# Interleaving the first slabs and computing six norms by square root, reciprocal and a Newton step

## What is computed

```
def rms_norm(x, g):
    xf = x.astype(jnp.float32)
    y = xf * lax.rsqrt(jnp.mean(xf * xf, axis=-1, keepdims=True) + EPS)
    return (y * g.astype(jnp.float32)).astype(x.dtype)

for i in range(DEPTH):              # DEPTH = 2
    h = rms_norm(x, g[0]); h = mlstm_mixer(h, ...) or short_conv_mixer(h, ...)
    x = x + rms_norm(h, g[1])
    h = sqrelu_mlp(rms_norm(x, g[2]), w_mlp_up[i], w_mlp_down[i])
    x = x + rms_norm(h, g[3])
```

## Time and profile before

| what | value |
| --- | --- |
| three runs | 954.48, 957.66, 964.06 us, median 957.66 |
| profiled execution | 954.73 us, of which the span of its instructions 952.9 us |
| mean granted TensorE clock | 0.993 |
| TensorE, VectorE, ScalarE, GpSimd busy | 99%, 68%, 56%, 10% |
| DMA | 172 MB, 181 GB/s |

### The profile page before, as it was taken

One profiled execution on the slowest core, in us unless ns is written; L12 is line 12 of the kernel. 1 busy time (PEld: TensorE's weight loads), 2 busy tenths in 40 slices (PEclk: granted clock), 3 DMA queues, 4 the chain that ended last, 5 costly groups with the idle time before them and its releaser, 6 DMA issues.

```text
span 952.9 us, 20117 instructions
## 1 busy us (share of the span) xinstructions
PE 942.0 (99%) x8046; PEld 934.3 (98%) x8046; DVE 644.4 (68%) x886; ACT 536.6 (56%) x757; POOL 100.0 (10%) x96
## 2 busy tenths in 40 slices
PE   9999999999999999999999999999999999999997
PEld 8999999999999999999999999999999999999997
DVE  5667687665444886688765444894765679999742
ACT  6566667654444555556655444565554566767542
POOL 0111100000000000109100000015120120000001
PEclk9999999999999999999999999999999999999998
DMA  8532646455554365545655553654342445556531
GB/s 330 226 133 94 222 173 221 177 198 199 188 209 177 121 226 185 177 177 185 214 180 213 181 195 120 250 212 143 133 177 99 167 177 188 210 181 216 191 119 45
DMA packets 26422, 172.20 MB, mean 181 GB/s; under 512 B 3444, under 2 KB 4084, under 8 KB 6136
## 3 DMA queue, kind: packets, MB, share of 16 engines
q1 hardware_dynamic: 26216, 171.04, 50.2%
q10 hardware_dynamic: 144, 0.26, 0.1%
HBM read 170.24 MB, written 1.05 MB: 180 GB/s over the span
## 4 chain that ended last, share of the span: by engine, by line
PE 92%; DVE 3%; ACT 2%; issue 1%; DMA 1%; SPq 0%; POOL 0%; POOLq 0%; ACTq 0%
PE po L434 26%; PE po L436 25%; PE po L435 25%; PE po L461 2%; PE po L463 2%; PE po L462 2%; PE third L434 2%; PE third L435 2%; PE third L436 2%; DVE wL L1358 2%; ACT wH L874 1%; DMA raw<-in_weights 1%; PE pc L790 1%; PE pn L528 1%; PE pn L518 0%
## 5 line engine op out<-in xcount | busy, mean ns | idle before, releaser
L1358 DVE TENSOR_TENSOR wL<-raw,wH 128x1024 fp32r<-128x1024 f32 x316 | 385.5, 1242 | 158.9 <-ACT wH L874 158.6
L874 ACT ACTIVATE wH<-raw 128x1024 fp32r<-128x1024 f32 x316 | 331.2, 1057 | 222.8 <-PE po L436 202.5
L434 PE MATMUL po<-xnH,wH 128*128 128x256 f32 x1296 | 364.6, 281 | 3.5 <-DVE wL L1358 1.5
L436 PE MATMUL po<-xnH,wL 128*128 128x256 f32 x1296 | 359.6, 277 | 0.0
L435 PE MATMUL po<-xnL,wH 128*128 128x256 f32 x1296 | 359.6, 277 | 0.0
L434 PEld LDWEIGHTS po<-xnH,wH 128*128 128x128 f32 x1296 | 244.5, 189 | 5.4 <-issue 2.8
L435 PEld LDWEIGHTS po<-xnL,wH 128*128 128x128 f32 x1296 | 244.4, 189 | 0.2
L436 PEld LDWEIGHTS po<-xnH,wL 128*128 128x128 f32 x1296 | 244.3, 189 | 0.0
L436 PE MATMUL po<-hH,wL 128*128 128x256 f32 x688 | 189.9, 276 | 0.0
L434 PE MATMUL po<-hH,wH 128*128 128x256 f32 x688 | 189.9, 276 | 0.0
L435 PE MATMUL po<-hL,wH 128*128 128x256 f32 x688 | 189.9, 276 | 0.0
(11 more groups left out here) (311 smaller groups left out, 1144.5 us busy)
## 6 DMA issues: line engine op xcount, KB each, us to landing
raw<-in_weights SPq DMA_DIRECT2D x157, 1024.0 KB, 4.8
raw<-in_weights SPq DMA_DIRECT2D x4, 256.0 KB, 5.2
raw<-in_weights SPq DMA_DIRECT2D x2, 512.0 KB, 7.5
mem<-in_memT SPq DMA_DIRECT2D x1, 1024.0 KB, 12.0
out<-y SPq DMA_DIRECT2D x4, 256.0 KB, 2.6
x<-in_xT SPq DMA_DIRECT2D x3, 256.0 KB, 5.5
decayt<-in_decay SPq DMA_DIRECT2D x1, 512.0 KB, 3.5
x<-in_xT ACTq DMA_DIRECT2D x1, 256.0 KB, 3.5
```

Of the source, the lines that this page charges most:

```text
L434: pe.matmul(psum[:, n, 0:T], wH[w][:, wc], aH[:, ac, :], start=start, stop=False)
L436: return pe.matmul(psum[:, n, 0:T], wL[w][:, wc], aH[:, ac, :], start=False, stop=stop)
L874: act.activation(wH[b % HL][:, hs], raw[b % RAW][:, hs], ACT.Copy).then_inc(s_hi, 1)
L1358: dve.tensor_tensor(wL[b % HL][:, hs], raw[b % RAW][:, hs], wH[b % HL][:, hs].bitcast(f32), ALU.subtract)\
```

## The change

**Start.** The second slab comes in quarters too, turn by turn with the first's. `first_slabs` runs both slabs chunk by chunk; the gate products and the sums of norm 0 stand further apart in the third slab.

**Norms 2, 3, 5, 6, 7, 8** (`rooted`). TensorE sums the squares with a 128 x 128 matrix of ones, so that the sum stands on all partitions and isn't spread later. ScalarE takes the square root and, apart, the mean square itself (`square_root`). VectorE takes the reciprocal of the root and improves it by one Newton step (`newton`): four operations of 128 x 256. `mean_square`, GpSimd's power, `norm_spread` and `keep_R` go for these norms. At a boundary the factor `Rpost` is then read from SBUF instead of PSUM. ScalarE loads the table with Sqrt at two places.

**Boundary before cin.** The pair of slabs goes by two chunks at a time (`slab_pair_by_twos`), the second slab's first quarter is split early, and the sums of norm 5 stand between the last chunks of the two slabs.

**Others.** In out2's last turn both halves of a split come after the residual and the feed. In the cross-attention some small products are moved together, and the `spacer`, a product whose result nobody reads, is two products in place of one.

```diff
--- before.py
+++ after.py
+        def rooted(n):
+
+            return n in (2, 3, 5, 6, 7, 8)
+
+        def powers(norm):
+            return sum(not rooted(n) for n in range(norm))
+
+        root, msq, step = sq[2][:, 0, :], sq[2][:, 1, :], sq[3][:, 0, :]
+        Rpost = sq[3][:, 1, :]
...
                 qs = slice(q * QUARTER, (q + 1) * QUARTER)
                 sp.dma_start(raw[0][:, qs], weights[0, :, qs]).then_inc(s_quarter[q], 16)
+                sp.dma_start(raw[1][:, qs], weights[1, :, qs]).then_inc(s_quarter1[q], 16)
                 if q < 3:
                     sp.dma_start(x[:, 2 * q + 2:2 * q + 4, :], xT[:, 2 * q + 2:2 * q + 4, :]).then_inc(s_x[q + 1], 16)
-            sp.dma_start(raw[1][:, 0:HALF], weights[1, :, 0:HALF]).then_inc(s_second, 16)
-            sp.dma_start(raw[1][:, HALF:], weights[1, :, HALF:]).then_inc(s_raw[1], 16)
-            sp.dma_start(par[:, C:], params[:, C:]).then_inc(s_par, 16)
...
-            def first_slab():
+            def first_slabs(between):
 
                 for k in range(8):
-                    if k % 2 == 0:
-                        pe.wait_ge(s_xn, k + 2)
-                        if k % 4 == 0:
-                            pe.wait_ge(s_qlo, k // 4 + 1)
-                        else:
-                            weights_ready(0, k // 4)
-                    for n in range(2):
-                        mm = products(slot(0), n, 0, k, xnH, xnL, k, k == 0, k == 7)
-                    if k == 3:
-                        mm.then_inc(s_half, 1)
-                mm.then_inc(s_slab, 1)
+                    pe.wait_ge(s_xn, k + 1)
+                    for j in range(2):
+                        if k % 2 == 0 and k < 6:
+                            pe.wait_ge(s_qlo, k + j + 1)
+                        elif k == 6:
+                            pe.wait_ge(s_lo, 2 * j + 2)
+                        for n in range(2):
+                            mm = products(slot(j), n, j, k, xnH, xnL, k, k == 0, k == 7)
+                        if k == 3:
+                            mm.then_inc(s_half, 1)
+                        if k == 7:
+                            mm.then_inc(s_slab, 1)
+                    if k in between:
+                        between[k]()
...
                 mm.then_inc(s_slab, 1)
+
+            def slab_pair_by_twos(name, aH, aL, feed, between):
+
+                s, g = SLAB0[name], GROUP0[name]
+                for kk in range(0, 8, 2):
+                    for j in range(2):
+                        if kk == 0:
+                            slot_free(g + j)
+                        if kk % 4 == 0 and (j, kk) != (1, 0):
+                            weights_ready(s + j, kk // 4)
+                        if (j, kk) == (1, 0):
+                            pe.wait_ge(s_two_lo, 1)
+                        if (j, kk) == (1, 2):
+                            weights_ready(s + j, 0)
+                        for k in (kk, kk + 1):
+                            if j == 0:
+                                pe.wait_ge(s_xn, 8 * feed + k + 1)
+                            for n in range(2):
+                                mm = products(slot(g + j), n, (s + j) % HL, k, aH, aL, k, k == 0, k == 7)
+                            if k == 3:
+                                mm.then_inc(s_half, 1)
+                            if k == 7:
+                                mm.then_inc(s_slab, 1)
+                        if kk + j in between:
+                            between[kk + j]()
...
                 else:
                     pe.wait_ge(s_sqa, squares_added(n + 1))
                 for t in range(TT):
-                    mm = pe.matmul(pn[:, t:t + 1], sq[0][:, 0, t * P:t * P + P], ones[:, 0:1], start=True, stop=True)
+                    tc = slice(t * P, t * P + P)
+                    if rooted(n):
+                        mm = pe.matmul(pn[:, P + t * P:2 * P + t * P], ones[:, :], sq[0][:, 0, tc], start=True, stop=True)
+                    else:
+                        mm = pe.matmul(pn[:, t:t + 1], sq[0][:, 0, tc], ones[:, 0:1], start=True, stop=True)
                 mm.then_inc(s_sum, 1)
 
             def norm_spread(n):
 
                 if n == 0:
                     pe.wait_ge(s_cst, 32)
-                pe.wait_ge(s_r, n + 1)
...
-                norm_sums(0)
-                gates(1, range(4))
-
-            phase_slab("qk", 1, xnH, xnL, between={6: lambda: gates(0, range(4)), 7: lambda: gates(0, range(4, 8))})
-            phase_slab("qk", 2, xnH, xnL, between={0: sums_and_gates, 1: lambda: gates(1, range(4, 8)), 3: lambda: norm_spread(0)})
+            first_slabs({6: lambda: gates(0, range(4)), 7: lambda: gates(0, range(4, 8))})
+            phase_slab("qk", 2, xnH, xnL, between={0: lambda: norm_sums(0), 2: lambda: gates(1, range(4)), 3: lambda: norm_spread(0), 5: lambda: gates(1, range(4, 8))})
             phase_slab("qk", 3, xnH, xnL, between={6: log_sums})
             phase_slab("v", 0, xnH, xnL, by_token=True, between={1: turn_a})
...
-            slab_pair("cin", xnH, xnL, 2, {6: lambda: norm_sums(5)})
+            slab_pair_by_twos("cin", xnH, xnL, 2, {6: lambda: norm_sums(5)})
...
 
+            def square_root(n):
+                act.wait_ge(s_sum, n + 1)
+                act.activation(root, pn[:, P:P + T], ACT.Sqrt, scale=1.0 / D, bias=eps).then_inc(s_root, 1)
+                act.activation(msq, pn[:, P:P + T], ACT.Identity, scale=1.0 / D, bias=eps).then_inc(s_msq, 1)
+
...
                 s = SLAB0[up]
+                if rooted(2 * post + 2):
+                    square_root(2 * post + 2)
                 if value is not None:
...
                     feed_squares(1)
                 else:
-                    split(s + 1, halves=(0,))
+
+                    b = s + 1
+                    act.wait_ge(s_raw[b % RAW], 16 * (b // RAW + (b % RAW > 1)))
+                    act.wait_ge(s_sum, 2 * post + 3)
+                    act.activation(wH[b % HL][:, 0:QUARTER], raw[b % RAW][:, 0:QUARTER], ACT.Copy).then_inc(s_two_hi, 1)
+                    act.wait_ge(s_half, b - 1)
...
 
-                split(s0 + 2)
+                split(s0 + 2, halves=(0,))
+                square_root(n_norm)
+                split(s0 + 2, halves=(1,))
                 split(s0 + 3)
-                keep_R(n_norm, Rs[:, :])
...
 
+            def newton(n, dst, done):
+
+                dve.wait_ge(s_root, sum(rooted(m) for m in range(n + 1)))
+                link(dve.reciprocal(dst, root))
+                link(dve.tensor_tensor(step, dst, dst, ALU.mult))
+                dve.wait_ge(s_msq, sum(rooted(m) for m in range(n + 1)))
+                link(dve.scalar_tensor_tensor(step, msq, -0.5, step, ALU.mult, ALU.mult))
+                k = dve.scalar_tensor_tensor(dst, step, 1.5, dst, ALU.add, ALU.mult)
+                if done is None:
+                    link(k)
+                else:
+                    k.then_inc(done, 1)
+
             def mean_square(n):
...
-                mean_square(n)
+                R = Rpost if rooted(n) else pn[:, P:P + T]
+                if rooted(n):
+                    newton(n, R, None)
+                else:
+                    mean_square(n)
                 split(first, halves=(1,))
+                b = first + 1
                 if two:
-                    split(first + 1, halves=(0,))
-                dve.wait_ge(s_R, n + 1)
+                    split(b, halves=(0,))
+                else:
+                    dve.wait_ge(s_two_hi, 1)
+                    dve.tensor_tensor(wL[b % HL][:, 0:QUARTER], raw[b % RAW][:, 0:QUARTER], wH[b % HL][:, 0:QUARTER].bitcast(f32),
+                                      ALU.subtract).then_inc(s_two_lo, 1)
+                    dve.wait_ge(s_R, powers(n + 1))
...
+                dve.tensor_tensor(y[:, 1, :], y[:, 1, :], R, ALU.mult).then_inc(s_t, 1)
                 dve.wait_ge(s_t, 4 * post + 1)
                 dve.tensor_tensor(x[:, 1, :], x[:, 1, :], y[:, 1, :], ALU.add).then_inc(s_xadd, 1)
                 feed_pair(feeds, 0, gain)
@@ -1605,15 +1694,17 @@
                     split(first + 2, halves=(1,))
                     add(3)
                 else:
-                    split(first + 1, halves=(0,))
                     scale(1)
                     add(1)
                     scale(2)
                     feed_pair(feeds, 1, gain)
+                    dve.wait_ge(s_hi, 2 * b + 1)
+                    dve.tensor_tensor(wL[b % HL][:, QUARTER:HALF], raw[b % RAW][:, QUARTER:HALF],
+                                      wH[b % HL][:, QUARTER:HALF].bitcast(f32), ALU.subtract).then_inc(s_lo, 1)
                     add(2)
-                    split(first + 1, halves=(1,))
+                    scale(3)
                     feed_pair(feeds, 2, gain)
-                    scale(3)
...
                     split(s, halves=(0,))
-                mean_square(n)
+                if rooted(n):
+                    newton(n, Rs[:, :], s_Rs)
+                else:
+                    mean_square(n)
```

(4 more changed lines are left out.)

87 lines of the change are left out of this document (53 added, 34 removed).

## The result

The changed kernel took 978.21 us (median of 5 runs, 973.59 to 985.45), the kernel before 957.66 us on the same chip (954.08 to 964.06). The ratio is 1.0227, with a 95% interval of 1.0176 to 1.0279. It is slower, as forecast, by more than forecast: 969 us had been predicted. The stated range, 953 to 980, holds it; the forecast's own range, 965 to 974, does not. The profiled execution took 984.16 us, its span 982.4 us.

The account below looks back on a forecast made before the run. TensorE, busy 99% of the span, was taken as the bound, with tight boundaries where VectorE delays it. The terms -3.5 + 9.6 + 5.0 - 0.8 + 4 = +14.3 on 954.7 gave 969 us, range 953 to 980.

Parts of the forecast that it names:

- Start, -3.5 us: At the start, interleaving the two first slabs removes three TensorE waits; slab 3 begins at 28.1 instead of 31.60 us.
- RECIPROCAL at 2.1 us, chain 3.6: In the six norms, RECIPROCAL of 256 columns takes 2.1 us, making VectorE's chain of four operations 3.6 us.
- rival (a): RECIPROCAL is as short as any other operation: chain 1.9 us, time 956 to 957, not slower; chance 0.22.
- The root on ScalarE, 0.43 us with hand-over: In the six norms, ScalarE's square root ahead of VectorE's chain takes 0.43 us including its hand-over.
- Boundaries, 3 x 3.2 us: At boundaries 0, 2 and 3 (norms 2, 6, 8), the first scaling comes 3.2 us later and shows in full: +9.6 us.
- Norms 3, 7 and 5, 1.7 + 1.7 + 1.6: In the blocks behind the boundaries, the chain delays the fourth slab (norms 3, 7) and cx in cin (norm 5): +5.0 us.
- Boundary before cin: The 1.1 us wait for the second slab's split goes, the clock should hold; the pair ends some 0.7 us earlier.
- Query projection, -0.8 us: In the query projection, moving both of the last slab's splits behind the residual and the feed saves 0.8 us.
- Half clock, three times 1.3 us: Behind each of the three boundaries, one half-clock spell follows the 3.4 us wait, at 1.3 us each: +4 us.
- rival (c): The slow matmul cadence stays without the spread to reset it; each MLP pays 5 us: 975 to 985; chance 0.08.
- (b): The clock holds through the three boundary waits: 965 us, with the scatter up to 968; chance 0.13.
- (d): VectorE has unseen slack, and starts, cin and the clock all gain with nothing lost: 947 us; chance 0.04.

Follow-up runs that it names:

- after_again: The changed kernel run once more with nothing edited: 977.47 us, ratio 1.0160 to the kernel before.
- all_powers: The changed kernel with all thirteen norms by GpSimd's power again, the rest of the change kept: 958.11 us, ratio 0.9964 to the kernel before.
- chain_later: The changed kernel with VectorE's chain for norms 3, 5 and 7 moved behind the three half splits: 982.95 us, ratio 1.0324 to the kernel before.
- no_newton_step: The changed kernel without the Newton step, the factor being the RECIPROCAL of the root: 961.93 us, ratio 1.0092 to the kernel before.
- no_reciprocal: The changed kernel with RECIPROCAL replaced by a SCALAR_TENSOR_TENSOR writing ones, the factor a constant: 967.13 us, ratio 1.0063 to the kernel before.
- resets: The changed kernel with all norms by powers plus an unread fp32 product in each turn of the long loops: 961.75 us, ratio 1.0088 to the kernel before.

## Why the prediction was right, and where it was off

*Start, -3.5 us.* Measured -2.2 by the start of slab 3 (29.44 for 31.60; 28.94 in after_again, 29.04 in all_powers). The clock held, as expected. But waits did not all go: 0.41 and 0.31 us are left in the changed kernel, 0.50 and 0.53 in all_powers. Two thirds of the starts in this stretch have the slow spacing in the changed kernel, under a third in the two others.

*RECIPROCAL at 2.1 us, chain 3.6.* Mis-sized: 1.75 and 3.16 us. The price of a column was nearly right, 6.5 ns for 6.25. What was too much is the rest: the sum put a whole TENSOR_TENSOR of 0.425 us under it, where the 153 ns of the shortest operation belong; 0.153 + 256 x 0.00625 = 1.753 us. Choosing the upper end was right, since the lower would have given rival (a). There was luck in it, since the 6.5 ns were the difference of two operations only 13 ns apart, which could as well have been a fixed cost. The Trainium skill ("VectorE: DVE Perf Modes", "First, the fixed hardware budget") says that Reciprocal is an iterative divide with a repeat count of 8. The estimate of 2.3 us read this as 8 cycles for each column. The rows give (1753 - 166) / 254 = 6.25 ns a column, which is six cycles of the 0.96 GHz that went into that estimate, so the trace does not agree with that reading.

*The root on ScalarE, 0.43 us with hand-over.* Mis-sized the other way: 0.475 us for Sqrt, and 0.51 from its start to RECIPROCAL's.

*Boundaries, 3 x 3.2 us.* The term that carries the sum, and right. VectorE's delay was to be 3.2 us and was 2.95. The wait was to be 3.4 us and was 3.58; the two errors, the chain taken too long and TensorE's earlier arrival left out of the wait, nearly cancel. Its place was right too, but half of the reading was missing: the delay also reaches the first slab's operand, which is late by 1 us, so that TensorE waits in two pieces.

*Norms 3, 7 and 5, 1.7 + 1.7 + 1.6.* Measured 1.57, 2.25 and 1.58 us (after_again), 5.4 for 5.0. The prediction put all of it at the fourth slab; more than half of norm 3's stood ahead of the third. That part of the chain is hidden in VectorE's idle time, which the prediction had read, is shown by chain_later.

*Boundary before cin.* The second slab's wait for its split (1.20 us from start to start before) is gone and the half clock with it, as forecast. The sums of norm 5 now wait 1.51 us from start to start, so the waits there are 2.4 us, where they were 2.0: as the prediction said, the pair ends with VectorE, and only the clock was gained.

*Query projection, -0.8 us.* The wait is gone from the profile.

*Half clock, three times 1.3 us.* There is one spell behind each of the three boundaries, 3.41 us long in after_again. It begins 0.59, 0.31 and 0.05 us before the second wait ends, and half of what is left of it is 1.4 to 1.7 us, 4.6 for the three where the term had 4. In the first profile two of them were 6.8 us long. What decides the clock is shown more closely than before: with a wait of 2.61 us (no_newton_step) all three boundaries had a spell, with 2.30 us (no_reciprocal) two of three, with 0.89 us none. It is not the length alone: at cin a wait of 3.30 us in chain_later had none.

*The sum.* +14.3 us was predicted on the profiled execution. after_again's span lies 15.0 us over the profile before, and its three losses explain it: +14.5 of waits, +2.4 of half clock, +0.3 of cadence, -2.2 in what remains. The mechanism and its price were right. Against a typical run of the kernel before, the half clock costs more than these 2.4 us: the profile before has spells at the start and before cin, which 17 of its 23 runs beside after_again, at a mean clock of 0.997 or 0.998 for the profile's 0.993, can hardly have had.

*Where the 9 us went.* The step that failed is the reading of the spacing: "There is a second, slower cadence, and in the trace it lasts until some fp32 matmul resets it". The prediction drew two things from it: that the spacer costs nothing, and rival (c), that the MLPs could be slow since the spread no longer resets them. There is no reset. A product switches, across a wait either may follow, and each loop of some 1440 matmuls is 6 us longer or not in each execution. (The slow spacing was misread too: 163 matmuls in 19 us give 116.6 ns, but from start to start it is 117.8, so a loop pays 6.4 us and not 5.) The sum was put on the profile before, 954.7 us, in which all three loops happened to be fast; the median of its chip was 957.7, and in the three later comparisons before had 960.4, 960.9 and 954.4. I left this offset of 3 us to the range instead of adding it.

The other 6 us are, as far as the runs tell, slow loops in the five runs of the changed kernel. Their span times mean clock is 966.0 to 971.6. Less the 952.3 us that its profile leaves without half clock and cadence, that is 14 to 19 us of cadence, 16 in the mean; the profile before had 5.7. This is an estimate, and it can be made for the kernel before as well, with 939.9 taken off: 16 us in the mean beside after_again, 15 beside all_powers, and 7 beside no_newton_step. So the changed kernel does not clearly meet the slow cadence more often than the one before. The profiles say the same: 4 of 20 MLP loops behind a norm in root form were slow and 0 of 6 behind one by the power (resets left aside), numbers too small to tell them apart. Beside after_again the difference of the two kernels is 15 us by the ratio and 16.5 by the medians, near the 14.3 of the sum; the 20.5 us of the first comparison are in part the luck of five runs.

Rival (a) was excluded by the duration, (b) by the spells. (c) gave the right number by the wrong mechanism. What decided against (d) is all_powers: with nothing lost the gain is 2 to 3 us, not 8.

## What to carry to other kernels

Before an operation is taken off a small engine and given to a busy one, look at what stands between its start and its use. Here 2.4 us of power and spread (121.38 to 123.77) lay behind two splits and cost nothing, while 3 us of chain in VectorE's queue cost, at the boundaries, a us of wait for each us, and the clock on top. RECIPROCAL costs 6.25 ns for each column: do it on the narrowest form of the data, which here was 128x2; no run here tried that for these norms. And where single executions of a program lie 6 us apart in steps, find the loop that makes the step before a difference between two kernels is read from one profile of each.

## What the runs showed of the hardware

Back-to-back matmuls of 256 columns have two cadences at full clock, 113.3 and 117.8 ns from start to start, and stay in one for over 1400 matmuls. A single small fp32 product between them switches from either one to the other (17 of 18 times), and so do two in a row (10 of 10); across a wait it changed in about half of the cases (44 of 92). How often a loop is slow differs between chips. What in TensorE or in its feed this is, no run here shows. RECIPROCAL costs 6.25 ns a column, against 425 ns in all for a TENSOR_TENSOR of 256 columns. Half clock did not follow the length of a wait alone: in one profile two waits of 2.30 us had it behind them and a third of 2.30 us did not, and one of 3.30 us at cin did not either.
